# Meta keys of a head pair turned together: block-diagonal values in a two-layer attention and feed-forward kernel

## The reference

```
s = jnp.concatenate([s_meta, s_win], axis=-1)
...
p = jnp.exp(s - m)
p = (p / (jnp.sum(p, axis=-1, keepdims=True) + jnp.exp(sk - m))).astype(v.dtype)
o = (jnp.einsum('bnhgqm,bmhd->bnqhgd', p[..., :META], vm)
     + jnp.einsum('bnhgqk,bnkhd->bnqhgd', p[..., META:], vb))
```

## Time and profile before

| | |
|---|---|
| time, median of 3 runs | 1752.04 us (1750.26 to 1752.36) |
| time of the profiled execution | 1752.92 us |
| its span in the trace | 1751.1 us |
| pairs of heads | 24 (12 in each layer) |
| value tiles turned | 12 (6 in each layer) |

### The profile page before, as it was taken

How to read it: one execution, slowest core, us unless ns; L and a number is a source line. 1 busy time by engine, 2 the same in 40 slices (tenths; PEclk the granted TensorE clock), 3 DMA queues, 4 the chain that set the end, 5 groups by cost and what they waited for, 6 DMA issues and landing times.

```text
span 1751.1 us, 36991 instructions
## 1 busy us (share of the span) xinstructions
PE 1724.7 (98%) x14000; PEld 1663.3 (95%) x14000; DVE 1173.0 (67%) x2053; ACT 819.6 (47%) x1316; POOL 259.8 (15%) x255
## 2 busy tenths in 40 slices
PE   9999999999999999999999999999999999999997
PEld 8899999999999998888999999999999788999997
DVE  6667756767665566665886655766566666787754
ACT  5555444444444433545554443444433455654443
POOL 0030000011000203333420001000111433340001
PEclk9999999999999999999999999999999999999999
DMA  7435555555555543332555555555554342555553
GB/s 269 142 112 183 184 180 184 188 183 179 176 172 175 174 162 128 121 124 103 167 181 173 172 176 169 180 170 168 180 174 153 107 157 97 169 181 189 182 183 131
DMA packets 84312, 288.80 MB, mean 165 GB/s; under 512 B 9072, under 2 KB 15984, under 8 KB 83952
## 3 DMA queue, kind: packets, MB, share of 16 engines
q1 hardware_dynamic: 79856, 283.14, 48.9%
q10 hardware_dynamic: 4352, 4.20, 0.8%
HBM read 285.96 MB, written 1.34 MB: 164 GB/s over the span
## 4 chain that ended last, share of the span: by engine, by line
PE 89%; DVE 6%; ACT 4%; issue 1%; DMA 0%; POOL 0%; SPq 0%; ACTq 0%; DVEq 0%
PE PS L861 27%; PE PS L863 27%; PE PS L862 27%; DVE w_lo L1513 2%; PE PS L1370 1%; PE PS L1334 1%; ACT S_all L737 1%; ACT w_hi L453 1%; PE PS L1374 1%; PE PS L1298 0%; PE PS L1342 0%; DMA raw<-stream 0%; PE PS L1055 0%; DVE PT L2099 0%; DVE PT L2098 0%
## 5 line engine op out<-in xcount | busy, mean ns | idle before, releaser
L1513 DVE TENSOR_TENSOR w_lo<-raw,w_hi 128x1024 fp32r<-128x1024 f32 x525 | 656.1, 1250 | 301.1 <-ACT w_hi L453 291.1
L861 PE MATMUL PS<-x_hi,w_hi 128*128 128x272 f32 (+1 forms) x2832 | 819.5, 289 | 2.3 <-DVE w_lo L1513 2.2
L863 PE MATMUL PS<-x_hi,w_lo 128*128 128x272 f32 (+1 forms) x2832 | 810.2, 286 | 0.0
L862 PE MATMUL PS<-x_lo,w_hi 128*128 128x272 f32 (+1 forms) x2832 | 808.2, 285 | 0.0
L453 ACT ACTIVATE w_hi<-raw 128x1024 fp32r<-128x1024 f32 x525 | 551.3, 1056 | 518.3 <-PE PS L863 512.7
L861 PEld LDWEIGHTS PS<-x_hi,w_hi 128*128 128x128 f32 x2832 | 535.4, 189 | 8.9 <-issue 4.2
L863 PEld LDWEIGHTS PS<-x_hi,w_lo 128*128 128x128 f32 x2832 | 535.7, 189 | 0.0
L862 PEld LDWEIGHTS PS<-x_lo,w_hi 128*128 128x128 f32 x2832 | 534.7, 189 | 0.7
L861 PE MATMUL PS<-a_hi,w_hi 128*128 128x272 f32 (+1 forms) x1280 | 364.8, 285 | 1.3 <-DVE a_lo L2136 1.3
L863 PE MATMUL PS<-a_hi,w_lo 128*128 128x272 f32 (+1 forms) x1280 | 363.8, 284 | 0.0
L862 PE MATMUL PS<-a_lo,w_hi 128*128 128x272 f32 (+1 forms) x1280 | 362.9, 284 | 0.0
(11 more groups left out here) (302 smaller groups left out, 1241.2 us busy)
## 6 DMA issues: line engine op xcount, KB each, us to landing
raw<-stream SPq DMA_DIRECT2D x525, 512.0 KB, 3.3
biasB<-rpbz ACTq DMA_DIRECT2D x16, 256.0 KB, 3.2
G<-b1mats SPq DMA_DIRECT2D x2, 1024.0 KB, 6.7
h<-xT SPq DMA_DIRECT2D x4, 272.0 KB, 5.5
out<-qk SPq DMA_DIRECT2D x4, 256.0 KB, 3.1
mat<-mats SPq DMA_DIRECT2D x1, 952.0 KB, 5.4
v_tok<-u_rows SPq DMA_DIRECT2D x4, 142.0 KB, 3.2
mat<-u_rows SPq DMA_DIRECT2D x4, 142.0 KB, 4.0
```

What stands on the lines that cost most here:

```text
L861: pe.matmul(ps, hi, rh, start=first, stop=False)
L862: pe.matmul(ps, hi, rl, start=False, stop=False)
L863: return pe.matmul(ps, lo, rh, start=False, stop=last)
L1513: dve.tensor_tensor(w_lo[:, slot, :], raw[:, slot, :], w_hi[:, slot, :].bitcast(F32), ALU.subtract).then_inc(lo_done, 1)
```

## The change

The probabilities of the meta keys of both heads go side by side into a new buffer `p_meta`, 32 columns for each query tile, so that two transposes of 32 columns take the place of four of 16. The values of the 16 meta keys then stand twice in `v_tok`, rows 0 to 15 with head 0's 64 columns and rows 16 to 31 with head 1's, zeros elsewhere, so that one product of 32 rows and 128 columns takes the place of two of 16 rows and 64 columns. To make these rows, DVE repeats the meta tokens in `vstage` (three times in all: the third copy, rows 32 to 47, is the plain one for the meta tokens' own queries), the third transpose of each value tile becomes a plain product with the identity, of 48 columns, and DVE multiplies its result by a mask `M_OWN`. The mask widens the constants by 128 columns.

```diff
--- before.py
+++ after.py
@@ -118,7 +118,10 @@
 M_ID, M_ONES, M_PA, M_PC = 0, P, 2 * P, 3 * P
 M_SEL16 = 4 * P
 M_SEL4 = M_SEL16 + 9 * 17
-M_TAB = M_SEL4 + 16
+M_OWN = M_SEL4 + 16
+M_TAB = M_OWN + P
+MV = 2 * META
+VS = SEQ + 3 * META
 M_MA = M_TAB + 4 * L
 NM = M_MA + 3 * L
 
@@ -176,12 +179,13 @@
         col = sb("col", [P, NC])
         mat = sb("mat", [P, NM])
         small = sb("small", [P, 256])
+        p_meta = sb("p_meta", [P, 2, 2, MV])
         router_w = sb("router_w", [P, KD, 20])
         PS = ctx.enter_context(nc.psum_tensor("PS", [P, 8, 512], F32))
 
         ident, ones = mat[:, M_ID:M_ID + P], mat[:, M_ONES:M_ONES + P]
         Gf = G[:, :, :].rearrange("p a b -> p (a b)")
-        vstage = [G[:, 6, :], G[:, 7, :]]
+        vstage = [Gf[:, 5 * L + VS * i:5 * L + VS * (i + 1)] for i in range(2)]
         acc, sq, ms = G[:, 20, :], G[:, 21, :], G[:, 22, :]
         half_acc, half_sq = G[:, 18, :], G[:, 19, :]
         zero = small[:, 1:2]
@@ -758,10 +762,10 @@
 
                     act.wait_ge(m_turned_out, l * 3 + m + 1)
                     if m == 1:
-                        act.activation(PTm[0:META, 0:192], PS[0:META, 6, 0:192], ACT.Copy).then_inc(m_probsT, 2)
+                        act.activation(PTm[MV:MV + META, 0:192], PS[0:META, 6, 0:192], ACT.Copy).then_inc(m_probsT, 2)
                         return
                     act.activation(PTm, PS[:, 6, 0:256], ACT.Copy).then_inc(m_probsT, 1)
-                    act.activation(PTm2[0:META, :], PS[0:META, 6, 256:384], ACT.Copy).then_inc(m_probsT, 1)
+                    act.activation(PTm2[MV:MV + META, :], PS[0:META, 6, 256:384], ACT.Copy).then_inc(m_probsT, 1)
 
                 def load_bias(p):
 
@@ -1301,7 +1305,8 @@
                             vs = vstage[i % 2]
                             pe.transpose(PS[:, b, 0:P], vs[:, 0:P], ident)
                             pe.transpose(PS[:, b, P:2 * P], vs[:, P:2 * P], ident)
-                            mm = pe.transpose(PS[0:META, b, 2 * P:3 * P], vs[:, 2 * P:L], ident)
+                            mm = pe.matmul(PS[0:3 * META, b, 2 * P:3 * P], vs[:, 2 * P:2 * P + 3 * META], ident,
+                                           start=True, stop=True, skip_group_check=True)
                         elif what == "sumC":
                             pe.wait_ge(c_squared, l * 5 + 5)
                             for e in range(5):
@@ -1354,10 +1359,8 @@
                     if p > 0:
 
                         pe.wait_ge(o_lo_done, l * PAIRS + p)
-                    for b in range(2):
-                        for qt in range(2):
-                            mm = pe.transpose(PS[0:META, 7, b * SEQ + qt * P:b * SEQ + (qt + 1) * P],
-                                              S4[:, p % 2, b, qt, SEQ:L], ident)
+                    for qt in range(2):
+                        mm = pe.transpose(PS[0:MV, 7, qt * P:(qt + 1) * P], p_meta[:, p % 2, qt, :], ident)
                     mm.then_inc(turned1_out, 1)
 
                 def pv(p):
@@ -1368,12 +1371,10 @@
                         for b in range(2):
                             vc = v_column(typ, t, b)
                             pe.matmul(PS[64 * b:64 * b + 64, 7, 0:SEQ], v_tok[:, kt, vc:vc + 64],
-                                      PT_b[b][:, kt * SEQ:(kt + 1) * SEQ], start=(kt == 0), stop=False)
-                    for b in range(2):
-                        vc = v_column(typ, t, b)
-                        mm = pe.matmul(PS[64 * b:64 * b + 64, 7, 0:SEQ], v_tok[0:META, 2, vc:vc + 64],
-                                       PT2[0:META, b * SEQ:(b + 1) * SEQ], start=False, stop=True)
-                    mm.then_inc(pv_out, 1)
+                                      PT_b[b][:, kt * SEQ:(kt + 1) * SEQ], start=(kt == 0), stop=False, skip_group_check=True)
+                    vc = v_column(typ, t, 0)
+                    pe.matmul(PS[:, 7, 0:SEQ], v_tok[0:MV, 2, vc:vc + P], PT2[0:MV, 0:SEQ], start=False, stop=True,
+                              skip_group_check=True).then_inc(pv_out, 1)
 
                 def m_scores(m):
 
@@ -1407,14 +1408,14 @@
                         for t in range(4):
                             for b in range(2):
                                 vc = v_column(1, t, b)
-                                mm = pe.matmul(PS[64 * b:64 * b + 64, 6, META * t:META * t + META], v_tok[0:META, 2, vc:vc + 64],
-                                               PTm[0:META, 48 * t + 32 * b:48 * t + 32 * b + META], start=True, stop=True)
+                                mm = pe.matmul(PS[64 * b:64 * b + 64, 6, META * t:META * t + META], v_tok[MV:MV + META, 2, vc:vc + 64],
+                                               PTm[MV:MV + META, 48 * t + 32 * b:48 * t + 32 * b + META], start=True, stop=True)
                     else:
                         for kt in range(3):
                             for b in range(2):
-                                vc, r = v_column(m, 0, b), P if kt < 2 else META
-                                probs = PTm[:, kt * P + 64 * b:kt * P + 64 * b + 64] if kt < 2 else PTm2[0:META, 64 * b:64 * b + 64]
-                                mm = pe.matmul(PS[64 * b:64 * b + 64, 6, 0:64], v_tok[0:r, kt, vc:vc + 64], probs,
+                                vc, r = v_column(m, 0, b), slice(0, P) if kt < 2 else slice(MV, MV + META)
+                                probs = PTm[:, kt * P + 64 * b:kt * P + 64 * b + 64] if kt < 2 else PTm2[r, 64 * b:64 * b + 64]
+                                mm = pe.matmul(PS[64 * b:64 * b + 64, 6, 0:64], v_tok[r, kt, vc:vc + 64], probs,
                                                start=(kt == 0), stop=(kt == 2))
                     mm.then_inc(m_pv_out, 1)
 
@@ -1985,9 +1986,13 @@
                     dve.wait_ge(chunk_used, cb + (c + t + 1))
                     n = nt if kind[0] == "q" else L
                     ps = PS[:, (bk + o + t) % 4, 0:n]
-                    dst = vstage[i % 2] if kind == "v" else qk[:, R_OF[kind] + i, 0:n]
+                    dst = vstage[i % 2][:, 0:L] if kind == "v" else qk[:, R_OF[kind] + i, 0:n]
                     if kind == "qB":
                         dve.scalar_tensor_tensor(dst, ps, 0.125, rstd[:, 0:n], ALU.mult, ALU.mult).then_inc(out_free, 1)
+                    elif kind == "v":
+                        step(dve.tensor_tensor(dst, ps, rstd[:, 0:n], ALU.mult))
+                        dve.tensor_copy(vstage[i % 2][:, L:VS].rearrange("p (r k) -> p r k", r=2),
+                                        dst[:, SEQ:L].unsqueeze(1).to_broadcast([P, 2, META])).then_inc(out_free, 1)
                     else:
                         dve.tensor_tensor(dst, ps, rstd[:, 0:n], ALU.mult).then_inc(out_free, 1)
                     for what, i in QKV_EVENTS.get(t, []):
@@ -2006,7 +2011,8 @@
                         elif what == "v":
                             step(dve.tensor_copy(v_tok[:, 0:2, i * P:(i + 1) * P],
                                                  PS[:, b, 0:2 * P].rearrange("p (k c) -> p k c", k=2)))
-                            dve.tensor_copy(v_tok[0:META, 2, i * P:(i + 1) * P], PS[0:META, b, 2 * P:3 * P])\
+                            dve.tensor_tensor(v_tok[0:3 * META, 2, i * P:(i + 1) * P], PS[0:3 * META, b, 2 * P:3 * P],
+                                              mat[0:3 * META, M_OWN:M_OWN + P], ALU.mult)\
                                .then_inc(aux_free, ax.up())
                         elif what == "sumC":
                             dve.tensor_scalar(G[0:10, 8, :], PS[0:10, b, 0:L], 1.0 / HD, EPS, ALU.mult, ALU.add)\
@@ -2096,7 +2102,7 @@
 
                     dve.wait_ge(turned1_out, l * PAIRS + p + 1)
                     dve.tensor_copy(PT_b[1], PS[:, 6, 0:512]).then_inc(probsT_dve, 1)
-                    dve.tensor_copy(PT2[0:META, :], PS[0:META, 7, 0:2 * SEQ]).then_inc(probsT_dve, 1)
+                    dve.tensor_copy(PT2[0:MV, 0:SEQ], PS[0:MV, 7, 0:SEQ]).then_inc(probsT_dve, 1)
 
                 def gate_out(j):
 
@@ -2272,8 +2278,10 @@
                     pool.wait_ge(rden_ready, l * PAIRS + s + 1)
                     for b in range(2):
                         i = 4 * (s % 2) + 2 * b
-                        tile = S4[:, s % 2, b, :, 0:L]
-                        pool.tensor_tensor(tile, tile, denp[:, i:i + 2].unsqueeze(2).to_broadcast([P, 2, L]),
+                        tile = S4[:, s % 2, b, :, 0:SEQ]
+                        pool.tensor_tensor(p_meta[:, s % 2, :, META * b:META * b + META], S4[:, s % 2, b, :, SEQ:L],
+                                           denp[:, i:i + 2].unsqueeze(2).to_broadcast([P, 2, META]), ALU.mult)
+                        pool.tensor_tensor(tile, tile, denp[:, i:i + 2].unsqueeze(2).to_broadcast([P, 2, SEQ]),
                                            ALU.mult).then_inc(probs_ready, 1)
 
                 ro = ob + (FFN_UP + KD + QKV_T + GATE_T)
@@ -2316,6 +2324,9 @@
     c[:, M_SEL16 + 17 * 8 + 16] = HD / 256
     for t in range(4):
         c[:, M_SEL4 + 4 * t + t] = 1.0
```

(3 more changed lines are left out.)

## The result

The changed kernel takes 1753.67 us (median of 20 executions, 1751.03 to 1757.12). The kernel before, on the same chip and in turn with it, takes 1752.01 us (20 executions, 1750.26 to 1752.83). The two medians are 1.7 us apart. The ratio estimated from all executions is 1.0013, with a 95% interval of 1.0007 to 1.0019: 2.3 us slower (1.2 to 3.3), where 1.8 us faster was forecast. The loss is within the 0.2% that was called no difference, but its interval leaves out no change.

A forecast was written before the change was run, and what follows sets the result against it. PE, busy for 98% of the span, was taken as the bound. Terms -5.2 - 0.3 - 1.2 + 4.9 gave -1.8 us, so 1750.2 us, no visible difference; the forecast's own range was 1748.3 to 1752.5, with quiet rivals 1745.8 to 1754.0.

The forecast's parts named there:

- 48 transposes fewer: Attention, turning of probabilities: two narrow transposes fewer per pair at 0.109 us each, 5.2 us off PE.
- shorter copy, on the waits: DVE's copy of turned meta rows, 0.25 us shorter: 0.03 us more gained in 11 pairs where PE waits, 0.3 us less.
- merged product: Attention, meta values: two full-width passes with 0.10 us around them in place of 0.15, 1.2 us less over 24 pairs.
- value turn as a plain product: Value preparation, 12 third turns: a second pass (0.11 us) and 0.30 us for few columns each, 4.9 us more.
- POOL's small products: POOL in attention: two extra small products, some 0.3 us more per pair, hidden, so nothing on the time.
- second rival: Merged product slower because its 128-column load shows: +2.4 us in place of -1.2, 1753.8 us, no difference; chance 0.10.
- first rival: Value turn: no drain, 48 columns handled like 128, costing 1.3 us; 1746.6 us, faster by 0.31%; chance 0.21.

The follow-up runs named there:

- e2: Changed kernel with the merged product split into two of 32 rows and 64 columns, side by side; 1752.77 us, one execution.
- e1: Changed kernel with the third turn of each value tile a transpose again, of 48 columns; 1749.00 us, ratio 0.9986 to the kernel before.
- e3: Changed kernel with the plain product of the value turn made 128 columns wide, the added columns unread; 1749.12 us, one execution.
- e4: Changed kernel with POOL's two large products first and the small ones behind both; 1752.83 us, one execution.
- e7: Changed kernel, unchanged, timed and profiled again; 1754.32 us, ratio 1.0013 to the kernel before.
- e13: Kernel before with the first transpose of each value tile done five times, 0.44 us more a tile; 1758.54 us, ratio 1.0043.
- e5: Changed kernel with the edits of e1, e2 and e4 together; 1745.20 us, ratio 0.9961 to the kernel before.
- e14: The kernel of e5 again on another chip; 1744.76 us, ratio 0.9965 to the kernel before.

## Why the prediction was wrong

Term by term, us, measured at an equal clock but for the last row:

| term | forecast | measured | from |
|---|---|---|---|
| 48 transposes fewer | -5.2 | -5.2 | timeline, 0.217 a pair |
| shorter copy, on the waits | -0.3 | -0.4 to -0.5, estimate | list of waits, 11 to 10; 0.05 each |
| merged product | -1.2 | +1.1 | 0.624 against 0.578, e2 |
| value turn as a plain product | +4.9 | +5.2 | e1, e3 |
| POOL's small products | 0 | +0.6 | e4 gives 0.8 back |
| sum | -1.8 | +1.2 | matched chunks |
| lower granted clock | not there | some +1.1 (0.0 to 2.1) | +2.3 less 1.2; e7 |

**The step that failed** is the merged product, forecast at 1.2 us less and measured at 1.1 us more. The prediction argued that "a pass of 0.215 hides such a load and one of 0.107 does not". It took 0.10 us for what surrounds the product; 0.19 was there (0.624 less 2 x 0.215). The load that shows is the first one, and no pass hides it: it begins 0.31 us behind the start of the last halved pass, after 0.38 us of idle time of the load queue, and at the same moment as the record of its own pass. From that pass's start to the next are 0.320 us, 0.105 more than the pass. In before and in e2, where the first load has 64 columns, the same distance is 0.267, 0.05 more than a pass, and in the earlier trace rows, with 10 columns, it is 0.234 where 0.229 is ordinary. The loads there take 0.18, 0.13 and 0.09 us. So the 0.10 around the product was read from a case whose load hardly shows, and carried to one whose load shows most. The 0.22 us behind the products of the earlier trace rows is the same distance behind another change of form, with a load of 128 columns, 0.10 above the ordinary: the row for it was in hand. Of the 3.0 us between sum and structure, 2.3 are this. The second rival named the load and had a tenth of the chance. Its upper end of 2.4 was too high: it added 0.10 to the pair of products as it was, and that pair already pays 0.05.

The measured 1753.67 us lies above the forecast's own 1748.3 to 1752.5 and almost on the second rival's 1753.8. That is partly luck. The rival's merged product was measured at +1.1 and not +2.4, and the rest of its time is the clock, which no case had.

**The value turn** was right in mechanism and size: e1 shows what the plain product costs and e3 that few columns are 0.32 of the 0.44 us, so the first rival fell. The Trainium skill, TensorEngine Tiling (Array Packing), Key Properties, says that a change of the tiling mode drains the engine; these runs agree (0.32 us with 48 columns, none with 128).

**POOL** was not the bound, and DVE's idle time hid nearly all of it, as forecast. "Nothing" failed only in the first pair of each layer, where there is no such idle time. I had read the steady step and not the first. The prediction's 0.3 us more POOL work a pair is also mis-added: two of 0.287 us less 6% of 2.14 or 3.50 are 0.36 to 0.45. Measured are 0.1, since POOL's busy time goes from 1717 ns a product to 1038 and 731.

**The clock** was no term of the sum, and by the middle of the timing's interval it makes up about half of the loss. That before and after differ in it is measured in 62 executions. That the longer value turns bring about the late falls is supported by e13, by the count of traces, 5 of 7 against 0 of 9, and by e5 and e14, which have no delay there and a clock of 0.996 to 0.997. It is not shown that they bring about the whole difference: e1 has no delay there, a mean clock of 0.9954 like after's, and a timed gain of 2.5 us where its structure gives 4.1. That the timed executions without a trace lose their time at the same place is argued, not shown. Two things stay open: why a few microseconds more in the value turns matter to the clock at all (the delay itself, or only the moment at which the 10*64 passes come), and what holds e1's clock down. Its one trace has only early falls, at 31.1 and 147.2 us.

## What to carry to other kernels

Count PE's passes by what stands at their edges: a plain product of few columns among full-width work cost 0.3 us here, more than a pass of 256 columns. Where the form changes in any case, as before the small products with the values, look at the width of the first load behind the change: two half-width products beat one full-width product that does half the work, by the 0.05 us that its wider load takes longer. Keep small turns as transposes, or make a plain product full width. When an edit is hidden by another engine's idle time, look for that idle time in the first step of a loop as well as in a steady one. And below 0.3%, compare traces stretch by stretch with the granted clock beside them: here the faster profiled execution belonged to the slower kernel.

## What the runs showed that was not expected

- The granted clock fell to 1.2 GHz in a kernel whose PE never stood idle around that moment, 0 to 1.3 us behind 2.4 us of passes of the form 10*64. Such a fall cost 1.5 us and was there in some executions and not in others of the same kernel.
- A small POOL product of 128x32 took 0.24 us alone and 1.22 us when it began while DVE's split was at work, five times as long. A large one of 128x512 that began ahead of a split kept its 1.03 us, and the split took 1.8 or 1.9 us where 1.2 is its time alone. In these rows the one that begins first keeps its time.
- The plain product of 48 columns was slower than the one of 128 by 0.32 us.
- A weight load of 32x128 took 0.05 us longer than one of 32x64, and behind a change of form the product around it took that much longer.
